# A kernel of two transformer blocks with an expert layer (PEER): which products the early expert tiles are made of, and which engine makes their rests

## The chip, the cores and the metric

The kernel runs on one core of a Trainium2 chip. Its time is the device time of one execution, in microseconds (us). Three executions of the kernel before took 1754.8 to 1755.04 us, median 1754.83.

## The reference, cut to what matters

Two blocks work on 256 tokens of width 1024. The second ends with an expert layer, PEER, which the change touches:

```python
q = (xb @ w_q).reshape(t, PEER_HEADS, 2, PEER_HALF)             # 8 heads, 2 halves of 128
s = jnp.einsum('thpd,hpkd->thpk', q, sub_keys)                  # 128 keys per half
top_s, top_i = lax.top_k(s, K)                                  # K = 16
cand_s = top_s[:, :, 0, :, None] + top_s[:, :, 1, None, :]
cand_i = top_i[:, :, 0, :, None] * PEER_N_KEYS + top_i[:, :, 1, None, :]
best_s, best_pos = lax.top_k(cand_s.reshape(t, PEER_HEADS, K * K), K)
idx = jnp.take_along_axis(cand_i.reshape(t, PEER_HEADS, K * K), best_pos, axis=-1)
gate = jax.nn.softmax(best_s, axis=-1)
h = jax.nn.gelu(jnp.einsum('thkd,td->thk', u_table[idx], xb), approximate=False)
return jnp.einsum('thk,thkd->td', gate * h, v_table[idx])
```

There are 128 x 128 = 16384 experts; all is float32.

## The kernel before, in words

The kernel doesn't gather rows of the tables. It multiplies all tokens with all of `u_table`, takes the gelu, multiplies by a weight that is zero for every expert that wasn't picked, and multiplies with all of `v_table`. Each table is cut into 128 tiles of 128 experts (512 KB each). This part, PEER, is the last: from about 975 us to the end at 1752 us.

**Exact products.** A float32 matrix is split into a top (rounded to the type fp32r, which TensorE takes at a high rate) and a rest (the matrix less its top). `three_passes` (L417) adds three products: top by top (L420), top by rest (L421), rest by top (L422). A tile of `u_table` so takes 8 x 3 matmuls of 128x256. The tokens' own top and rest are made once. A tile's pass through the engines is: SP starts its DMA into one of four slots of the ring (`expert_w`), ACT casts it to its top (`top_expert`, L2900), POOL (GpSimd) or DVE (VectorE) subtracts (the rest: L3113 on POOL, L3048 on DVE), PE (TensorE) multiplies, ACT takes the gelu from the bank into `hidden` (L2920; behind the hand-over L2927). SP starts the DMA of tile n when PE has begun tile n - 3; ACT casts tile n after the gelu of tile n - 3.

**Plain tiles.** Eight early tiles, `PLAIN` (6, 15, 17, 20, 30, 38, 41, 44), are multiplied as plain float32 matmuls (`plain_tile`, L2782), 8 of 128x256, without cast and rest. For them the tokens' rows are kept a second time, turned and not rounded: `x_turned`, made by 16 transposes of PE (L2771) and four copies of ACT (L2915), right behind the scores.

**The order of the stage.** PE first computes queries and scores (L2761), then the first `EARLY` = 46 tiles alone ("early tiles"). Meanwhile DVE picks, for each of two groups of 128 tokens (t = 0, 1; `pick_dve`): 16 heads of keys, five instructions each over 128 values (L2965 to L2969); a cast (L2978); the sums of all pairs (L2980, 128x2048); 8 heads of picks over 256 values; and for each of two digits of the picked position a shift or mask (L2988), a cast (L2989), an equality (L2990), a product (L2993) and a reduction (L2995), the last three over 2048 values. It ends with a copy (L2997), a subtraction (L2998) and, after t = 1, a memset (L3012) that posts `best_ready`.

**The hand-over.** `MERGED` is the order of the rest, written out as letters, and PE, ACT and DVE all follow it. "E": ACT, after the gelu of the last early tile, waits for `best_ready`, loads another table and takes the exponential (L2949). Then four more tiles "T"; "P": PE turns the picks and their weights (L2831) as soon as DVE has posted `picks_ready`, and ACT copies them; two tiles; then 64 groups "G" of four tokens, for which DVE makes masks (L3038, L3041), PE multiplies them (L2809) and DVE scales `hidden` (L3055), with the remaining tiles strewn between them. POOL makes the rests of the first `POOL_TILES` = `EARLY` + 6 tiles that aren't plain, DVE those of the others (L3048). Behind the last group, 128 tiles of `v_table` follow at 12 matmuls of 128x512 each.

**Buffers.** PSUM banks go round in two sets of four, `A` and `V`; `take` waits until a bank was emptied, `get` until it was filled. An engine's instructions run in the order written, so whatever waits holds up all behind it on that engine.

Of the kernel before, what the change touches and what calls it, by code (L numbers as in the profile page):

```python
# [14 lines left out]
ALU = mybir.AluOpType  # L15
ACT = mybir.ActivationFunctionType
F32 = mybir.dt.float32
# [5 lines left out]
P = 128  # L23
# [13 lines left out]
EARLY = 46  # L37
WEIGHT_UNIT = 2.0 ** 15
PLAIN = (6, 15, 17, 20, 30, 38, 41, 44)
# [156 lines left out]
def program(nc, dram, out, where):  # L196

    ctx = ExitStack()
    with ctx:
# [2465 lines left out]
        NH2 = 2 * PH  # L2665
# [29 lines left out]
        x_turned = hidden[:, EARLY + 6:EARLY + 14, :].rearrange("p j s -> p (j s)").rearrange("p (t k s) -> p t k s", t=TT, s=P)  # L2695
# [31 lines left out]
        def split_no(tile):  # L2727

            return tile + 1 - len([p for p in PLAIN if p < tile])
# [15 lines left out]
        def peer_pe(pe):  # L2745
# [21 lines left out]
            for t in range(TT):  # L2767
                for k in range(0, KT, 4):
                    bank = A.take(pe)
                    for j in range(4):  # L2770
                        ins = pe.transpose(bank[:, j * P:(j + 1) * P], xh[:, t, (k + j) * P:(k + j + 1) * P], ident)  # L2771
                    ins.then_inc(A.done, 1)
            mixed = Count()

            def plain_tile(tile):

                bank = A.take(pe)
                slot = tile % E_SLOTS
                pe.wait_ge(expert_landed[slot], 16 * (tile // E_SLOTS + 1))
                w = expert_w[:, slot, :].rearrange("p (k n) -> p k n", k=KT)  # L2780
                for k in range(KT):
                    ins = pe.matmul(bank[:, 0:S].rearrange("p (t s) -> p t s", t=TT), w[:, k, :], x_turned[:, :, k, :],  # L2782
                                    start=(k == 0), stop=(k == KT - 1))
                    if k == 0:
                        ins.then_inc(expert_begun, 1)
                ins.then_inc(A.done, 1)

            def u_tile(tile):
                bank = A.take(pe)
                slot = tile % E_SLOTS  # L2790
                if tile < POOL_TILES:
                    pe.wait_ge(u_split, split_no(tile))
                else:
                    pe.wait_ge(u_split_dve, tile - POOL_TILES + 1)
# [18 lines left out]
            for tile in range(EARLY):  # L2813
                if tile == PLAIN[0]:
                    A.evacuated_but(pe, 4)
                if tile in PLAIN:
                    plain_tile(tile)
                else:
                    u_tile(tile)
# [58 lines left out]
        def peer_act(act):  # L2878
# [9 lines left out]
            def top_expert():  # L2888

                n = tops.n  # L2890
                if tops.term is None and n in PLAIN:
                    tops.n += 1
                    return
# [76 lines left out]

        def pick_dve(dve, t):
            vec = nc.vector
            await_mark(dve, f"scores{t}")
            for h in range(NH2):
                ins = top16_dve(top_s[:, h, :], top_i[:, h, :], scores[:, t, h, :], spare_key[:, h, :])
            v(ins)
# [8 lines left out]
            v(ins)  # L2985

            for c, (op, by) in enumerate(((ALU.logical_shift_right, 4), (ALU.bitwise_and, 15))):
# [4 lines left out]
                                    ALU.is_equal))  # L2992
                v(vec.tensor_tensor(one_hot, one_hot, top_f[:, :, c, :].unsqueeze(2).broadcast_to([P, PH, TOPK, TOPK]),  # L2993
                                    ALU.mult))
                v(vec.tensor_reduce(key_no[:, t, c], one_hot, AX_X, ALU.add))  # L2995
# [6 lines left out]
        def peer_dve(dve):  # L3002
# [42 lines left out]
            def u_rest_dve(tile):  # L3045
                dve.wait_ge(expert_top_ready, split_no(tile))
# [61 lines left out]
        def peer_pool(pool):  # L3108
# [7 lines left out]
            for tile in range(POOL_TILES):  # L3116
                if tile not in PLAIN:
                    u_rest(tile)
# [196 lines left out]
```

## Time and profile before

| | |
|---|---|
| median of three runs | 1754.83 us |
| the profiled execution, its own time | 1754.11 us |
| its span | 1752.3 us |
| granted clock of TensorE | 0.996 of full |
| PE busy | 1703.8 us, 97% |
| DVE busy | 1134.7 us, 65% |
| ACT busy | 791.2 us, 45% |
| POOL busy | 348.8 us, 20% |
| matmuls | 12858 |
| chain of waits, by engine | PE 87%, DVE 5%, DMA 3%, ACT 2%, POOL 1% |

The span is the profiled execution from its first to its last instruction, 1.8 us shorter than its time. Busy times are per engine and may overlap. The chain of waits follows the work that ended last back to what released it. "Idle before" is the time that an engine stood before an instruction, with the one that ended it. A matmul row is pipelined: the next one begins before it ends, so the begin of a tile to the begin of the next is what a tile costs.

### The profile page before, as it was taken

How to read it: one execution, taken by the hardware profiler on the slowest of the kernel's cores; microseconds unless marked ns; L12 is line 12 of the kernel's file. 1: busy time of each engine (PE TensorE's matmuls, PEld its weight loads, DVE VectorE, ACT ScalarE, POOL GpSimd, SP SyncE). 2: the span in 40 equal slices, each digit the busy share in tenths (PEclk: the TensorE clock that was granted, in tenths of full speed). 3: DMA queues.
4: the chain of work that ended last, by engine and by line, in shares of the span. 5: the costliest groups of instructions: out<-in, count | busy, mean ns of one | idle time of the engine just before them, and what ended most of it. 6: DMA issues, size and time to landing. Idle time of an engine off the chain costs nothing.

```text
span 1752.3 us, 32963 instructions
## 1 busy us (share of the span) xinstructions
PE 1703.8 (97%) x12858; PEld 1514.6 (86%) x12858; DVE 1134.7 (65%) x1857; ACT 791.2 (45%) x1241; POOL 348.8 (20%) x325
## 2 busy tenths in 40 slices
PE   6999999999999999999899999999999999999997
PEld 2999879877999889877869999999999988888886
DVE  4877557677565465883664699488899644444444
ACT  4443445655544354551234534555544433333334
POOL 2000010111000010000010477600000155555553
PEclk9999999999999999999999999999999999999999
DMA  9878655456555534441044455545555566666664
GB/s 354 279 269 303 212 197 169 145 193 226 196 199 183 193 130 140 150 145 50 3 169 146 131 170 181 168 152 160 159 157 159 172 195 194 192 192 192 192 192 166
DMA packets 64385, 314.42 MB, mean 179 GB/s; under 512 B 7152, under 2 KB 7568, under 8 KB 44688
## 3 DMA queue, kind: packets, MB, share of 16 engines
q1 hardware_dynamic: 62928, 305.94, 52.3%
q10 hardware_dynamic: 1280, 6.82, 1.1%
q8 instruction: 85, 1.39, 0.3%
q14 instruction: 28, 0.23, 0.0%
q0 software_dynamic: 64, 0.04, 0.0%
HBM read 311.72 MB, written 1.05 MB: 178 GB/s over the span
## 4 chain that ended last, share of the span: by engine, by line
PE 87%; DVE 5%; DMA 3%; ACT 2%; POOL 1%; issue 1%; SPq 0%; DVEq 0%; POOLq 0%; ACTq 0%
PE bank L420 25%; PE bank L421 24%; PE bank L422 24%; DMA ring<-in_stream 2%; PE bank L2809 2%; DVE ring_rounded L381 1%; DMA ring<-in_experts 1%; POOL ring_rounded L3113 1%; PE bank L1351 1%; PE bank L2367 1%; PE bank L2782 1%; PE bank L781 1%; PE bank L2380 1%; PE bank L2018 1%; PE bank L595 0%
## 5 line engine op out<-in xcount | busy, mean ns | idle before, releaser
L422 PE MATMUL bank<-yb_rounded,ring_rounded 128*128 128x256 f32 x2000 | 566.4, 283 | 0.0
L2900 ACT CAST ring_rounded<-ring 128x1024 fp32r<-128x1024 f32 x248 | 260.5, 1051 | 279.2 <-DMA ring<-in_experts 279.2
L422 PEld LDWEIGHTS bank<-yb_rounded,ring_rounded 128*128 128x128 f32 x2000 | 384.2, 192 | 0.0
L381 DVE TENSOR_TENSOR ring_rounded<-ring,arena_rounded 128x1024 fp32r<-128x1024 f32 x230 | 270.8, 1220 | 132.6 <-ACT arena_rounded L367 132.0
L420 PE MATMUL bank<-yb_rounded,arena_rounded 128*128 128x256 f32 x1104 | 316.3, 287 | 1.7 <-DVE yT_rounded L897 1.3
L421 PE MATMUL bank<-yT_rounded,arena_rounded 128*128 128x256 f32 x1104 | 313.4, 284 | 0.0
L420 PE MATMUL bank<-yb_rounded,ring_rounded 128*128 128x256 f32 x960 | 278.2, 290 | 2.7 <-DVE ring_rounded L3048 1.7
L3075 DVE TENSOR_TENSOR ring_rounded<-ring,ring_rounded 128x1024 fp32r<-128x1024 f32 x128 | 156.8, 1225 | 190.5 <-ACT ring_rounded L2900 190.5
L367 ACT CAST arena_rounded<-ring 128x1024 fp32r<-128x1024 f32 x230 | 229.0, 1048 | 108.4 <-PE bank L420 99.8
L421 PE MATMUL bank<-yT_rounded,ring_rounded 128*128 128x256 f32 x960 | 271.2, 283 | 0.0
L421 PE MATMUL bank<-ring_rounded,arena_rounded 128*128 128x512 f32 x688 | 267.8, 389 | 0.0
L420 PEld LDWEIGHTS bank<-yb_rounded,arena_rounded 128*128 128x128 f32 x1104 | 212.9, 193 | 5.9 <-issue 4.0
L421 PEld LDWEIGHTS bank<-yT_rounded,arena_rounded 128*128 128x128 f32 x1104 | 212.9, 193 | 1.0 <-issue 1.0
L420 PE MATMUL bank<-ring_rounded,arena_rounded 128*128 128x512 f32 x512 | 199.4, 389 | 0.7 <-POOL arena_rounded L3131 0.7
L422 PE MATMUL bank<-ring_rounded,arena_rounded 128*128 128x512 f32 x512 | 199.3, 389 | 0.0
L420 PEld LDWEIGHTS bank<-yb_rounded,ring_rounded 128*128 128x128 f32 x960 | 183.6, 191 | 4.5 <-issue 4.3
L421 PEld LDWEIGHTS bank<-yT_rounded,ring_rounded 128*128 128x128 f32 x960 | 183.8, 191 | 0.1
L3128 POOL CAST arena_rounded<-field 128x256 fp32r (+1 forms) x128 | 94.7, 740 | 389.6 <-PE bank L420 389.6
L409 POOL TENSOR_TENSOR arena_rounded<-field,arena_rounded 128x1024 fp32r<-128x1024 f32 x8 | 23.0, 2896 | 704.8 <-ACT arena_rounded L401 704.8
L421 PEld LDWEIGHTS bank<-ring_rounded,arena_rounded 128*128 128x128 f32 x688 | 129.2, 188 | 27.2 <-issue 0.7
L3113 POOL TENSOR_TENSOR ring_rounded<-ring,ring_rounded 128x1024 fp32r<-128x1024 f32 x44 | 113.5, 2586 | 109.7 <-ACT ring_rounded L2900 109.6
L420 PEld LDWEIGHTS bank<-ring_rounded,arena_rounded 128*128 128x128 f32 x512 | 96.1, 188 | 21.1 <-issue 1.1
(439 smaller groups left out, 2651.4 us busy)
## 6 DMA issues: line engine op xcount, KB each, us to landing
ring<-in_stream SPq DMA_DIRECT2D x144, 1024.0 KB, 4.9
ring<-in_experts SPq DMA_DIRECT2D x256, 512.0 KB, 3.5
field<-in_stream SPq DMA_DIRECT2D x24, 512.0 KB, 7.1
field<-in_stream SPq DMA_DIRECT2D x4, 1024.0 KB, 6.9
field<-in_gains ACTq DMA_DIRECT2D x3, 512.0 KB, 7.8
field<-in_gains ACTq DMA_DIRECT2D x1, 1536.0 KB, 6.6
const<-in_const SPq DMA_DIRECT2D x1, 1473.0 KB, 11.2
xh<-in_x ACTq DMA_DIRECT2D x1, 1024.0 KB, 5.6
```

Of the source, the lines that this page charges most:

```text
L367: nc.scalar.copy(top, ring[:, g % SLOTS, half * HALF:(half + 1) * HALF]).then_inc(sem("weight_top_ready"), 1)
L381: ins = nc.vector.tensor_tensor(ring_r[:, g % SLOTS, half], ring[:, g % SLOTS, half], top.bitcast(F32), ALU.subtract)
L409: nc.gpsimd.tensor_tensor(rest[:, half], whole[:, half], top.bitcast(F32), ALU.subtract).then_inc(sem(f"own_split_{tag}"), 1)
L420: first = pe.matmul(bank, s_top, m_top, start=start, stop=False)
L421: pe.matmul(bank, s_top, m_rest, start=False, stop=False)
L422: return first, pe.matmul(bank, s_rest, m_top, start=False, stop=stop)
L781: ins = pe.matmul(bank[32 * k:32 * k + 32, :], silu_c[:, 4 * c + k, :], w[:, k, :], start=(c == 0), stop=(c == 1 and k > 0))
L2809: ins = pe.matmul(bank[:, q * P:(q + 1) * P], weighted[:, g % 2, q, i, :], masks[:, g % 2, q, 1, :], start=(i == 0), stop=(i == 1))
L2900: nc.scalar.copy(expert_top[:, n % E_SLOTS, :], expert_w[:, n % E_SLOTS, :]).then_inc(expert_top_ready, 1)
L3075: vec.tensor_tensor(expert_rest[:, slot, :], expert_w[:, slot, :], expert_top[:, slot, :].bitcast(F32), ALU.subtract).then_inc(v_split, 1)
L3113: nc.gpsimd.tensor_tensor(expert_rest[:, slot, :], expert_w[:, slot, :], expert_top[:, slot, :].bitcast(F32), ALU.subtract).then_inc(u_spl ...
L3128: nc.gpsimd.tensor_copy(h_top[:, b, :], src).then_inc(h_top_ready, 1)
```

## The change

It does four things.

1. `PLAIN`, `plain_tile`, `x_turned`, its 16 transposes and its four copies are gone. All 128 tiles of `u_table` go through `three_passes`.
2. Eight early tiles, `BETWEEN_PICKS` = (3, 9, 14, 19, 24, 30, 35, 41), have their rests made by DVE in `rest_between`, at fixed places in `pick_dve`: behind heads 4 and 14 of the keys, head 3 of the picks, the first equality and the second product of t = 0; behind head 7 of the keys, the sums and head 5 of the picks of t = 1. They have a semaphore of their own, for which PE waits. POOL makes the other rests.
3. `EARLY` is 48 and not 46, `POOL_TILES` 54 and not 52. POOL so makes 46 rests and not 44, DVE makes 74 and not 76 in the merged part.
4. ACT casts the eight tiles too. The counts for which rests wait become `tile + 1`.

Cut to its core (the counts in `v_rests` and `u_rest_dve`, and POOL's `tile not in PLAIN`, which becomes `tile not in BETWEEN_PICKS`, are left out):

```diff
-EARLY = 46
+EARLY = 48
-PLAIN = (6, 15, 17, 20, 30, 38, 41, 44)
+BETWEEN_PICKS = (3, 9, 14, 19, 24, 30, 35, 41)
...
-            for t in range(TT):
-                for k in range(0, KT, 4):
-                    bank = A.take(pe)
-                    for j in range(4):
-                        ins = pe.transpose(bank[:, j * P:(j + 1) * P], xh[:, t, (k + j) * P:(k + j + 1) * P], ident)
-                    ins.then_inc(A.done, 1)
...
-            def plain_tile(tile):
-
-                bank = A.take(pe)
-                slot = tile % E_SLOTS
-                pe.wait_ge(expert_landed[slot], 16 * (tile // E_SLOTS + 1))
-                w = expert_w[:, slot, :].rearrange("p (k n) -> p k n", k=KT)
-                for k in range(KT):
-                    ins = pe.matmul(bank[:, 0:S].rearrange("p (t s) -> p t s", t=TT), w[:, k, :], x_turned[:, :, k, :],
-                                    start=(k == 0), stop=(k == KT - 1))
...
             def u_tile(tile):
                 bank = A.take(pe)
                 slot = tile % E_SLOTS
-                if tile < POOL_TILES:
-                    pe.wait_ge(u_split, split_no(tile))
+                if tile in BETWEEN_PICKS:
+                    pe.wait_ge(sem("u_split_between"), BETWEEN_PICKS.index(tile) + 1)
+                elif tile < POOL_TILES:
+                    pe.wait_ge(u_split, pool_split_no(tile))
...
             for tile in range(EARLY):
-                if tile == PLAIN[0]:
-                    A.evacuated_but(pe, 4)
-                if tile in PLAIN:
-                    plain_tile(tile)
-                else:
-                    u_tile(tile)
+                u_tile(tile)
...
-            for t in range(TT):
-                for k in range(0, KT, 4):
-                    bank = A.get(act)
-                    nc.scalar.copy(x_turned[:, t, k:k + 4, :], bank[:, :].rearrange("p (j s) -> p j s", j=4)
-                                   ).then_inc(A.free, 1)
...
+        def rest_between(dve, tile):
+
+            dve.wait_ge(expert_top_ready, tile + 1)
+            slot = tile % E_SLOTS
+            nc.vector.tensor_tensor(expert_rest[:, slot, :], expert_w[:, slot, :], expert_top[:, slot, :].bitcast(F32),
+                                    ALU.subtract).then_inc(sem("u_split_between"), 1)
+
+        AFTER_KEYS = {(0, 4): 3, (0, 14): 9, (1, 7): 30}
+        AFTER_PICKS = {(0, 3): 14, (1, 5): 41}
+        AFTER_DIGITS = {(0, 0, "equal"): 19, (0, 1, "chosen"): 24}
...
             for h in range(NH2):
                 ins = top16_dve(top_s[:, h, :], top_i[:, h, :], scores[:, t, h, :], spare_key[:, h, :])
-            v(ins)
+                if h == NH2 - 1:
+                    v(ins)
+                if (t, h) in AFTER_KEYS:
+                    rest_between(dve, AFTER_KEYS[t, h])
...
+            if t == 1:
+                rest_between(dve, 35)
```

The order that this makes, at three places. PE, between the scores and the first expert tile; before (L2761 the scores, L2771 the transposes, L420 to L422 the first products of tile 0):

```order
L422 MATMUL bank<-yb_rounded,ring_rounded 128x256
L420 MATMUL bank<-yb_rounded,arena_rounded 128x256
L421 MATMUL bank<-yT_rounded,arena_rounded 128x256
L422 MATMUL bank<-yb_rounded,ring_rounded 128x256
L2761 MATMUL bank<-ring,field 128x128 x32
L2771 MATMUL bank<-const,xh 128x128 x16
L420 MATMUL bank<-yb_rounded,ring_rounded 128x256
L421 MATMUL bank<-yT_rounded,ring_rounded 128x256
```

In the changed kernel the row of L2771 is gone and nothing stands in its place. DVE, at the digits of t = 0, before (L2988 shift or mask, L2990 equality, L2993 product, L2995 reduction):

```order
L2988 TENSOR_SCALAR field<-field 128x128
L2989 CAST field<-field 128x128
L2990 TENSOR_TENSOR field<-field,const 128x2048
L2993 TENSOR_TENSOR field<-field 128x2048
L2995 TENSOR_REDUCE field<-field 128x128
L2988 TENSOR_SCALAR field<-field 128x128
L2989 CAST field<-field 128x128
L2990 TENSOR_TENSOR field<-field,const 128x2048
L2993 TENSOR_TENSOR field<-field 128x2048
L2995 TENSOR_REDUCE field<-field 128x128
L2997 COPY field<-field 128x8
```

The same place in the changed kernel, whose line numbers are 12 or 8 lower here; L2944 is the subtraction of `rest_between`:

```order
L2976 TENSOR_SCALAR field<-field 128x128
L2977 CAST field<-field 128x128
L2978 TENSOR_TENSOR field<-field,const 128x2048
L2944 TENSOR_TENSOR ring_rounded<-ring,ring_rounded 128x1024
L2983 TENSOR_TENSOR field<-field 128x2048
L2987 TENSOR_REDUCE field<-field 128x128
L2976 TENSOR_SCALAR field<-field 128x128
L2977 CAST field<-field 128x128
L2978 TENSOR_TENSOR field<-field,const 128x2048
L2983 TENSOR_TENSOR field<-field 128x2048
L2944 TENSOR_TENSOR ring_rounded<-ring,ring_rounded 128x1024
L2987 TENSOR_REDUCE field<-field 128x128
```

The first L2944 is the rest of tile 19, the second that of tile 24; each stands behind a wait for ACT's cast of its tile. The third place is head 5 of the picks of t = 1, in the changed kernel (L2934 to L2938 are the five instructions of a head):

```order
L2937 MAX field<-field 128x8
L2938 MAX_INDEX field<-field 128x8
L2944 TENSOR_TENSOR ring_rounded<-ring,ring_rounded 128x1024
L2934 MAX field<-field 128x8
L2935 MAX_INDEX field<-field 128x8
L2936 MATCH_REPLACE field<-field 128x256
L2937 MAX field<-field 128x8
```

That is the rest of tile 41. Behind it, to the end of the early tiles, DVE makes no rest; the digits of t = 1 stand as before.

## Rows read from the trace of the kernel before

**Rows 1.** The page, busy time, share of the span and instructions of each engine

```profile
PE 1703.8 (97%) x12858; PEld 1514.6 (86%) x12858; DVE 1134.7 (65%) x1857; ACT 791.2 (45%) x1241; POOL 348.8 (20%) x325
```

**Rows 2.** Waits of PE, 970 to 1752 us: who, for whom, total us, times, longest

```profile
PE bank L420 <- DVE ring_rounded L3048: 1.7, 1, 1.7
PE bank L420 <- POOL ring_rounded L3113: 0.7, 3, 0.3
```

**Rows 3.** Timeline of PE, 980 to 984 us: start, us, engine, line, operation

```profile
982.01 1.91 PE L2771 MATMUL bank<-const,xh 128*128 128x128 f32 x16
983.68 0.36 PE L420 MATMUL bank<-yb_rounded,ring_rounded 128*128 128x256 f32 x1
```

**Rows 4.** Timeline of ACT: gelus, begun as their tiles end, and a table load

```profile
989.71 0.38 ACT L2920 ACTIVATE field<-bank 128x256 f32<-128x256 f32 x1 [1.39 <-PE bank L422]
...
1001.23 0.38 ACT L2920 ACTIVATE field<-bank 128x256 f32<-128x256 f32 x1 [0.86 <-PE bank L422]
...
1010.43 0.38 ACT L2920 ACTIVATE field<-bank 128x256 f32<-128x256 f32 x1 [0.88 <-PE bank L422]
...
1013.70 0.38 ACT L2920 ACTIVATE field<-bank 128x256 f32<-128x256 f32 x1 [1.18 <-PE bank L422]
...
1059.06 0.38 ACT L2920 ACTIVATE field<-bank 128x256 f32<-128x256 f32 x1 [0.92 <-PE bank L422]
...
1061.94 0.38 ACT L2920 ACTIVATE field<-bank 128x256 f32<-128x256 f32 x1 [0.86 <-PE bank L422]
...
1124.68 1.28 ACT L2949 ACT_TABLE_LOAD   x1
...
1134.78 0.38 ACT L2927 ACTIVATE field<-bank 128x256 f32<-128x256 f32 x1 [0.79 <-PE bank L422]
```

**Rows 5.** Timelines of SP, ACT, POOL and PE: the life of tile 26

```profile
1053.56 0.33 SPq L3197 DMA_DIRECT2D ring<-in_experts  x1
...
1057.10 1.05 ACT L2900 CAST ring_rounded<-ring 128x1024 fp32r<-128x1024 f32 x1 [0.53 <-DMA ring<-in_experts]
...
1058.22 2.41 POOL L3113 TENSOR_TENSOR ring_rounded<-ring,ring_rounded 128x1024 fp32r<-128x1024 f32 x1 [0.30 <-ACT ring_rounded L2900]
...
1061.74 0.28 PE L420 MATMUL bank<-yb_rounded,ring_rounded 128*128 128x256 f32 x1
```

**Rows 6.** Timeline of DVE, 1026 to 1034 us: equality and product of the digits

```profile
1026.72 2.29 DVE L2990 TENSOR_TENSOR field<-field,const 128x2048 f32<-128x2048 f32 x1
1029.05 4.33 DVE L2993 TENSOR_TENSOR field<-field 128x2048 f32<-128x2048 f32 x1
```

**Rows 7.** Timeline of POOL, 1028 to 1041 us: the rests of tiles 16 and 19

```profile
1028.11 3.12 POOL L3113 TENSOR_TENSOR ring_rounded<-ring,ring_rounded 128x1024 fp32r<-128x1024 f32 x1 [3.29 <-ACT ring_rounded L2900]
...
1036.62 4.19 POOL L3113 TENSOR_TENSOR ring_rounded<-ring,ring_rounded 128x1024 fp32r<-128x1024 f32 x1 [0.88 <-ACT ring_rounded L2900]
```

**Rows 8.** DVE's digit and cast lines: times executed, duration ns min/median/max

```profile
L2993 DVE TENSOR_TENSOR field<-field x4: 2291/3310/4371, 1029.0 to 1105.8; 128x2048 f32<-128x2048 f32 x4
...
L2988 DVE TENSOR_SCALAR field<-field x4: 226/1038/2314, 1026.2 to 1100.9; 128x128 uint32<-128x128 uint32 x4
...
L2989 DVE CAST field<-field x4: 227/228/230, 1026.5 to 1103.2; 128x128 f32<-128x128 uint32 x4
...
L2997 DVE COPY field<-field x2: 170/1210/2249, 1045.3 to 1110.4; 128x8 f32<-128x8 f32 x2
...
L2978 DVE CAST field<-field x2: 293/686/1079, 1004.7 to 1071.1; 128x256 f32<-128x256 uint32 x2
```

**Rows 9.** Timeline of DVE: where its picking begins, and its last instruction

```profile
979.52 0.29 DVE L2965 MAX8 field<-field 128x8 f32<-128x128 f32 x1 [11.91 <-ACT field L2908]
...
1113.08 0.06 DVE L3012 MEMSET small<- 128x1 f32 x1
```

**Rows 10.** Waits of all engines, 975 to 1145 us: VectorE's for the exponential

```profile
DVE field L3015 <- ACT field L2949: 13.3, 1, 13.3
```

**Rows 11.** Line L3048, rests of merged tiles on DVE: duration ns min/median/max

```profile
L3048 DVE TENSOR_TENSOR ring_rounded<-ring,ring_rounded x76: 1212/1215/1227, 1142.0 to 1387.4; 128x1024 fp32r<-128x1024 f32 x76
```

More of the change, by code:

```diff
@@ L2692, in program @@
         denom = take(TT * PH).rearrange("p (t h) -> p t h", t=TT)
-        x_turned = hidden[:, EARLY + 6:EARLY + 14, :].rearrange("p j s -> p (j s)").rearrange("p (t k s) -> p t k s", t=TT, s=P)
         pick_weights = field[:, HID:HID + S]
@@ L2725, in program, with pool_split_no @@
         MERGED = ["E"] + ["T"] * 4 + ["P"] + ["T"] * (BEFORE - 4)
-        def split_no(tile):
-            return tile + 1 - len([p for p in PLAIN if p < tile])
+        def pool_split_no(tile):
+            return tile + 1 - len([p for p in BETWEEN_PICKS if p < tile])
         for m in range(GROUPS):
@@ L2890, in top_expert @@
                 n = tops.n
-                if tops.term is None and n in PLAIN:
-                    tops.n += 1
-                    return
                 full = 16 * (n // E_SLOTS + 1)
@@ L2984, in pick_dve @@
                 ins = top16_dve(best[:, t, h, :], pos[:, h, :], flat[:, h, :], spare_sum[:, h, :])
-            v(ins)
+                if h == PH - 1:
+                    v(ins)
+                if (t, h) in AFTER_PICKS:
+                    rest_between(dve, AFTER_PICKS[t, h])
             for c, (op, by) in enumerate(((ALU.logical_shift_right, 4), (ALU.bitwise_and, 15))):
@@ L2992, in pick_dve @@
                                     ALU.is_equal))
+                if (t, c, "equal") in AFTER_DIGITS:
+                    rest_between(dve, AFTER_DIGITS[t, c, "equal"])
                 v(vec.tensor_tensor(one_hot, one_hot, top_f[:, :, c, :].unsqueeze(2).broadcast_to([P, PH, TOPK, TOPK]),
                                     ALU.mult))
+                if (t, c, "chosen") in AFTER_DIGITS:
+                    rest_between(dve, AFTER_DIGITS[t, c, "chosen"])
                 v(vec.tensor_reduce(key_no[:, t, c], one_hot, AX_X, ALU.add))
@@ L3045, in u_rest_dve @@
             def u_rest_dve(tile):
-                dve.wait_ge(expert_top_ready, split_no(tile))
+                dve.wait_ge(expert_top_ready, tile + 1)
                 slot = tile % E_SLOTS
@@ L3073, in v_rests @@
                 mixed.n += 1
-                dve.wait_ge(expert_top_ready, mixed.at(NKEY - len(PLAIN) + mixed.n))
+                dve.wait_ge(expert_top_ready, mixed.at(NKEY + mixed.n))
                 vec.tensor_tensor(expert_rest[:, slot, :], expert_w[:, slot, :], expert_top[:, slot, :].bitcast(F32),
@@ L3111, in u_rest @@
                 slot = tile % E_SLOTS
-                pool.wait_ge(expert_top_ready, split_no(tile))
+                pool.wait_ge(expert_top_ready, tile + 1)
                 nc.gpsimd.tensor_tensor(expert_rest[:, slot, :], expert_w[:, slot, :], expert_top[:, slot, :].bitcast(F32),
@@ L3116, in peer_pool @@
             for tile in range(POOL_TILES):
-                if tile not in PLAIN:
+                if tile not in BETWEEN_PICKS:
                     u_rest(tile)
```

3 lines of the change are left out of this document (removed).

## The prediction

> **What bounds the kernel now.** I read the page's busy times first, then PE's waits, then the timelines of the early tiles. PE is busy 97% of the span [rows 1], and from 970 us to the end it waits for little: 1.7 us once for DVE's first rest of the merged part, 0.7 us for POOL [rows 2]. So PE's own work is the time, and what is taken off it counts in full as long as nobody becomes late. Two gelus that follow each other without a stall show what a tile of three passes costs: 1061.94 - 1059.06 = 2.88 us [rows 4].
>
> How much room the others have shows in the life of tile 26 [rows 5]: DMA issued 1053.56, cast from 1057.10 for 1.05, rest on POOL from 1058.22 for 2.41, done 1060.63; PE begins the tile at 1061.74. Its slack is 1.1 us. POOL has 2.4 us of work per 2.88 us. Whatever delays a rest by over 1.1 us stalls PE.
>
> **What delays rests: POOL and DVE shut each other out.** DVE's equality runs 1026.72 to 1029.01 [rows 6]. POOL's rest begun at 1028.11 takes 3.12 and not 2.4, to 1031.23, 2.2 after the equality's end [rows 7]. DVE's product, begun at 1029.05, takes 4.33 and not 2.29, to 1033.38, which is 2.15 after POOL's end. Whoever comes second stands until the other's whole instruction is over, and they take turns. DVE's smaller one-source instructions stand too: shift or mask 0.23 or up to 2.31, copy 0.17 or 2.25, cast over 256 values 0.29 or 1.08; two of four products are 2.0 too long, like rest 19 on POOL with 4.19 [rows 7, 8]. Summed, DVE stood for POOL six times, 2.04 + 2.08 + 1.62 + 2.08 + 2.08 + 0.79 = 10.7 us.
>
> **The sum, part by part** (against the profiled execution's 1754.1 us).
>
> Gone from PE: the transposes, 983.68 - 982.01 = 1.67 us [rows 3]. ACT's four copies behind them go too; ACT had room, so 0.
>
> Plain against three passes: the gelus at 1001.23 and 1010.43 enclose plain tile 6 and two others, 9.20 us, where three tiles of 2.88 take 8.64 [rows 4]. So 0.56 each, 8 of them: 4.5 us. Off PE in all: 6.2 us.
>
> Stalls that may go: between the gelus of tiles 1 and 49, at 989.71 and 1134.78, lie 48 tiles and 145.1 us; 48 x 2.88 + 8 x 0.56 = 142.7. The difference, 2.3 us with the roundings, is stalls (tile 9's gelu at 1013.70 comes 3.27 after the one before it) [rows 4].
>
> The two tiles that become early, with POOL's two more rests and DVE's two fewer in the merged part, leave PE's work as it is: 0. DVE's single wait of 1.7 us sits behind "P", whose order is unchanged: it stays.
>
> So with nobody late: 1754.1 - 6.2 - 2.3 = 1745.6.
>
> Added to DVE: eight rests of 1.22 [rows 11] = 9.8 us. DVE picks from 979.52 to 1113.1 [rows 9] and then waits 13.3 us [rows 10], so this alone fits. But a rest takes two tensors from SBUF like the equality and the product, so I count it as one that POOL shuts out; no row has such a rest meet POOL. And the plain tiles 15, 17, 20 and 41, 44 are gone, in whose time POOL stood idle beside DVE's digits. I work it forward: tile n due at 982.0 + 2.88 n plus earlier stalls; DMA issued 0.5 behind the begin of tile n - 3 and landing 3.5 later as for tile 26; cast 1.05; rest 2.4; turns as above.
>
> - Keys and sums of t = 0: rests 3 and 9 come in time. DVE's cast stands 2.3 for POOL's rest 10 (before: 0.8), the sums then hold up rest 11: tile 11 stalls 1.1.
> - First digit: before, the equality began at 1026.7 [rows 6]. Now three rests (3.6), a wait for a cast (0.4), the longer cast wait (1.5) and a turn of POOL (2.5) come first: 1034.6. Rest 19 runs 1036.9 to 1038.1, tile 19 was due at 1037.8: stall 0.3, and tile 21 0.9.
> - Second digit: product 1038.1, waits 2.2, ends 1042.5; reduction 1044.8; mask and cast stand a turn of 2.2 each, 1049.8; equality 1052.1; product 1054.5; rest 24 stands 2.2 and ends 1057.9. Tile 24 was due at 1053.3: **stall 4.4**.
> - t = 1: rest 30 in time, rest 35 late by 1.2, rest 41 in time.
> - Digits of t = 1, no tile spared: where equality and product follow each other, a rest takes 2.3 + 2.2 = 4.5 per 2.88. Less the slack for the first: about 1.0 + 1.5 for each digit, 5.0.
> - DVE's own turns there make six waits of 2.2. It ends at 1139.3, 26.2 later than before: 9.8 of rests, 1 of waits for casts, 15.4 more for POOL. ACT, at 1124.7 for "E" before [rows 4], gets there at about 1133.9 and stands 5.4 us; its cast of tile 51 is behind it. 1.3 of it is absorbed, since ACT is three tiles ahead: tile 51 stalls 4.1.
>
> New stalls: 1.1 + 0.3 + 0.9 + 4.4 + 1.2 + 5.0 + 4.1 = 17.0. 1745.6 + 17.0 = 1762.6, and 0.5 for ten restarts of PE, 1763.1: 9.0 more than before. The three runs' median is 0.7 above the profiled time, so I forecast 1763.8.
>
> Bounds. If neither rests nor small instructions stand for POOL any more than before, 1747 (the last rival). If the DMAs land later (4.5 us) or rest 35 too meets POOL (2.2 more), 1766 to 1769. The cast L2989 never met POOL, four times 0.23 [rows 8]; I take it like the longer cast, which did. The Trainium skill, "Advanced Engine Details and Errata", section "Mode Summary", says that GpSimd and two-port VectorE instructions block each other and lists casts among the latter; by it the sum stays, and if L2989 didn't stand it would be 0.9 less.
>
> **The rivals.** A difference under 0.2%, 3.5 us, is about what a measurement of this kernel can't tell from none.
>
> *Fewer turns (0.12).* DVE's small instructions slip in between POOL's instead of standing for each. For it: in rows 8 half of them took 0.23. Against: they met nobody then. Without their waits DVE is some 10 us earlier, rest 24 is nearly in time and "E" hardly waits: new stalls of 12, +3 to +5, 1758.
>
> *Relief and new stalls cancel (0.10).* The change doesn't do what it says: moving rests to DVE does not relieve, since each still takes the same turn, but the stalls stay near 8.5 us. 1752 to 1758, say 1755. Trainium skill, "Perfetto Trace Analysis", section "Optimizing Scalar/DVE Operations": as the two share a read port, offloading between them "might not help".
>
> *Faster (0.14).* The places are just right. Shift DVE's places of before by 1.2 us per rest already made, and each of the eight falls between its tile's cast and 1.3 us before its tile is due (rest 19: 1029.0 + 3.7 = 1032.7, cast 1032.8, needed 1036.7). Then POOL is idle in the widest meetings, DVE's waits stay at 10.7 us, it ends at 1123.5, "E" waits 1 to 2 us: 1745.6 + 2 = 1747.5. It decides at tile 24: DVE has 2.5 us of room there, one extra turn of 2.2. A second one flips it. Against: my working finds four by then.
>
> **How the numbers follow.** The forecast case, +5 to +15, has 0.64; of fewer turns about two thirds are over +3.5. Slower: 0.64 + 0.08 = 0.72; same 0.13; faster 0.15. The range 1752 to 1769 holds the forecast case up to its late DMAs, fewer turns and most of the cancelling case; the fast case is left out.
>
> **What would show it.** Right: product (now L2983) and casts of 2.2 us and more, over ten of them; DVE's rest for tile 24 taking 3.4 and not 1.22 or begun behind 1052; PE waits for DVE L2944 and POOL of 15 us in all; DVE waiting for the exponential not 13.3 us but next to nothing, and ACT waiting for DVE at L2949's place; `best_ready`'s memset near 1139. First products at 982.0 and no L2771 confirm the 1.7; gelus 2.88 apart where nobody stalls the 4.5. Wrong: the memset near 1123, DVE's waits near 10 us, and PE's stalls under 4 us; then the time is 1747, and the step that failed is the count of turns.

## The result, and the profile after

The changed kernel takes **1764.36 us** (median of 5 runs, 1762.31 to 1767.11) beside 1754.8 for the kernel before on the same chip: ratio 1.0053, 95% interval 1.0041 to 1.0064, slower by 9.3 us (7.2 to 11.2). The forecast was 1763.8. The profiled execution was the slowest of the five: it took 1767.11, its span is 1763.9.

The page's busy times of the change, beside [rows 1]:

```profile
PE 1702.9 (97%) x12906; PEld 1517.3 (86%) x12906; DVE 1155.7 (66%) x1861; ACT 797.1 (45%) x1243; POOL 358.5 (20%) x327
```

PE is busy 0.9 us less than before, though more than that was taken off it: busy time also grows where its clock is low, so what a part costs is read from the starts of tiles below. What grew are waits. The waits of the changed kernel, 970 to 1180 us (engine, its instruction, whom it waited for, total us, times, longest), beside [rows 2, 10]:

```profile
PEld bank L420 <- issue: 12.5, 6, 4.1
PE bank L420 <- POOL ring_rounded L3105: 8.5, 6, 2.4
...
ACT field L2918 <- DVE small L3004: 4.3, 1, 4.3
PE bank L420 <- DVE ring_rounded L2944: 3.9, 1, 3.9
DVE ring_rounded L2944 <- ACT ring_rounded L2874: 3.2, 3, 1.3
...
PE bank L420 <- DVE ring_rounded L3040: 1.8, 1, 1.8
...
DVE field L3007 <- ACT field L2918: 0.5, 1, 0.5
```

PE waits 8.5 us for POOL where it waited 0.7, and 3.9 for one rest of DVE (L2944 is `rest_between`). DVE's 13.3 us of waiting for the exponential are 0.5, and ACT waits 4.3 for DVE. The rows don't add up to a cost: a stall shows on PE and on its weight loads both. So from here on a **stall** is read from PE's timeline: the start of a tile, less that of the tile before, less 2.88 us.

DVE's lines of the picking in the change (busy us, mean ns of one, idle before), where [rows 8] had means of 1154 for the shift and 228 for the cast, as L2988 and L2989:

```profile
L2983 DVE TENSOR_TENSOR field<-field 128x2048 f32<-128x2048 f32 x4 | 15.5, 3873 | 0.1
L2944 DVE TENSOR_TENSOR ring_rounded<-ring,ring_rounded 128x1024 fp32r<-128x1024 f32 x8 | 11.8, 1474 | 3.3 <-ACT ring_rounded L2874 3.2
L2976 DVE TENSOR_SCALAR field<-field 128x128 uint32<-128x128 uint32 x4 | 9.5, 2370 | 0.1
...
L2963 DVE TENSOR_TENSOR field<-field 128x2048 f32<-128x2048 f32 x2 | 6.7, 3334 | 0.1
L2977 DVE CAST field<-field 128x128 f32<-128x128 uint32 x4 | 5.2, 1292 | 0.1
L2989 DVE COPY field<-field 128x8 f32<-128x8 f32 x2 | 2.4, 1216 | 0.1
```

All four shifts and masks stood a whole turn of POOL. The timeline of DVE around the digits of t = 0 (start us, us) shows the chain of turns that ends in tile 24, and the last instruction of the picking:

```profile
1045.38 2.35 DVE L2976 TENSOR_SCALAR field<-field 128x128 uint32<-128x128 uint32 x1
1047.77 2.38 DVE L2977 CAST field<-field 128x128 f32<-128x128 uint32 x1
1050.18 2.29 DVE L2978 TENSOR_TENSOR field<-field,const 128x2048 f32<-128x2048 f32 x1
1052.51 2.29 DVE L2983 TENSOR_TENSOR field<-field 128x2048 f32<-128x2048 f32 x1
1054.83 3.25 DVE L2944 TENSOR_TENSOR ring_rounded<-ring,ring_rounded 128x1024 fp32r<-128x1024 f32 x1
...
1141.50 0.06 DVE L3004 MEMSET small<- 128x1 f32 x1
```

And PE's timeline at tile 24, which waits for that rest of 3.25 us:

```profile
1054.01 0.28 PE L422 MATMUL bank<-yb_rounded,ring_rounded 128*128 128x256 f32 x1
1058.23 0.55 PE L420 MATMUL bank<-yb_rounded,ring_rounded 128*128 128x256 f32 x1 [3.94 <-DVE ring_rounded L2944]
1058.58 0.41 PE L421 MATMUL bank<-yT_rounded,ring_rounded 128*128 128x256 f32 x1
1058.80 0.41 PE L422 MATMUL bank<-yb_rounded,ring_rounded 128*128 128x256 f32 x1
```

The matmuls behind the idle come 0.21 to 0.22 us apart and not 0.12. The stretches show why (length, busy time of PE, PEld, DVE, ACT, POOL, then PE's granted clock):

```profile
1058.20:1063.50 5.30, 5.27 (x25) 5.30 (x26) 5.03 (x17) 0.00 (x0) 2.12 (x1) 0.50 0.32 102
1063.50:1070.00 6.50, 6.50 (x55) 6.50 (x55) 6.06 (x33) 3.14 (x5) 3.58 (x2) 0.99 0.53 161
```

Tile 24 ran at a clock of 0.50, 1.2 GHz, took 5.26 us, and tile 25 had the full clock again. Idle 3.94 us, PE lost 2.4 more.

The chain of waits between 1030 and 1145 us, its shares by line, is headed by a line of DVE's; in the kernel before, PE's L420 led there with 16.4% and the highest of DVE's had 1.2%:

```profile
by line: DVE field L2983 13.4%; PE bank L420 11.4%; PE bank L422 10.7%; PE bank L421 10.7%; DVE field L2976 8.3%; DVE field L2978 8.0%; DMA ring<-in_experts 7.7%; DVE field L2987 6.0%; DVE ring_rounded L2944 5.0%; DVE field L2977 4.5%; ACT 
```

**The ledger** of the two profiled executions. The products of the scores start at 974.86 before and 975.37 after (0.5 us of difference, ahead of what was changed). With 46 early tiles in place of 48, the kernel before has done two more groups (L2809, 0.50 us each) when it starts tile 54; they are taken off, so that both sides have done the same.

| term | predicted | found |
|---|---|---|
| transposes, first expert product behind the scores' start | -1.67 | 8.81 to 7.07: -1.7 |
| eight tiles of three passes | -4.5 | -4.5 |
| old stalls gone | -2.3 | -2.4 |
| tile 11 | 1.1 | 1.4 |
| tiles 19, 21 | 0.3, 0.9 | 0.1, 0.9 |
| tile 24, the wait | 4.4 | 4.1 |
| tile 24, the clock | none | 2.4 |
| tile 35 | 1.2 | 0.6 |
| tiles 44, 45, 48, 49 | 5.0 | 5.5 |
| tile 51 ("E") | 4.1 | 2.5 |
| restarts, stalls under 0.1 | 0.5 | 0.6 |
| up to the start of tile 54 | +9.0 | +9.4 |
| behind the start of tile 54 | 0 | +1.7 |

0.5 + 9.4 + 1.7 are the 11.6 us between the two spans; the two executions' times are 13.0 apart, the medians of the runs 9.6. So the ledger has more to explain than the medians show.

Most of the last row can be read from the trace. PE at the start of tile 54 in the change, and at tile 52 before, which stands at the same place of the order; then the stretches of the two tiles:

```profile
1159.02 0.39 PE L420 MATMUL bank<-yb_rounded,ring_rounded 128*128 128x256 f32 x1 [1.83 <-DVE ring_rounded L3040]
```
```profile
1143.36 0.36 PE L420 MATMUL bank<-yb_rounded,ring_rounded 128*128 128x256 f32 x1 [1.75 <-DVE ring_rounded L3048]
```
```profile
1159.00:1163.40 4.40, 4.38 (x24) 4.40 (x24) 3.72 (x5) 0.00 (x0) 0.00 (x0) 0.61 0.36 119
```
```profile
1143.30:1146.30 3.00, 2.94 (x25) 2.93 (x25) 2.96 (x5) 0.26 (x1) 0.00 (x0) 1.00 0.49 131
```

Both stand there for DVE's first rest of the merged part, but in the change the clock then fell: from this tile to the next are 4.86 us, before 3.37. That is 1.5 of the 1.7.

### The profile page after: what moved, and what is told of

Read it like the earlier page. It is cut to its first block, busy times and chain, and to the rows that moved or that the text cites. A ratio compares the mean times of both kernels' runs of the same rounds, so it can differ in the third digit from the quotient of the medians.

```text
span 1763.9 us, 33078 instructions
## 1 busy us (share of the span) xinstructions
PE 1702.9 (97%) x12906; PEld 1517.3 (86%) x12906; DVE 1155.7 (66%) x1861; ACT 797.1 (45%) x1243; POOL 358.5 (20%) x327
## 4 chain that ended last, share of the span: by engine, by line
PE 84%; DVE 10%; DMA 3%; ACT 2%; issue 1%; POOL 0%; SPq 0%; DVEq 0%; POOLq 0%; ACTq 0%
PE bank L420 24%; PE bank L421 23%; PE bank L422 23%; DMA ring<-in_stream 2%; PE bank L2791 2%; DVE ring_rounded L381 1%; DMA ring<-in_experts 1%; DVE field L2983 1%; PE bank L1351 1%; PE bank L2367 1%; PE bank L781 1%; PE bank L2380 1%; DVE field L2976 1%; DVE field L2978 1%; PE bank L2018 1%
## 5 line engine op out<-in xcount | busy, mean ns | idle before, releaser
L422 PE MATMUL bank<-yb_rounded,ring_rounded 128*128 128x256 f32 x2064 | 586.2, 284 | 0.0
L2874 ACT CAST ring_rounded<-ring 128x1024 fp32r<-128x1024 f32 x256 | 268.9, 1051 | 294.6 <-DMA ring<-in_experts 294.6
L422 PEld LDWEIGHTS bank<-yb_rounded,ring_rounded 128*128 128x128 f32 x2064 | 398.4, 193 | 0.0
L420 PE MATMUL bank<-yb_rounded,arena_rounded 128*128 128x256 f32 x1104 | 316.7, 287 | 1.6 <-DVE yT_rounded L897 1.3
L420 PE MATMUL bank<-yb_rounded,ring_rounded 128*128 128x256 f32 x1024 | 297.4, 290 | 15.2 <-POOL ring_rounded L3105 8.5
L421 PE MATMUL bank<-yT_rounded,ring_rounded 128*128 128x256 f32 x1024 | 291.0, 284 | 0.0
L420 PEld LDWEIGHTS bank<-yb_rounded,arena_rounded 128*128 128x128 f32 x1104 | 213.5, 193 | 5.3 <-issue 3.8
L420 PEld LDWEIGHTS bank<-yb_rounded,ring_rounded 128*128 128x128 f32 x1024 | 197.7, 193 | 17.0 <-issue 12.5
L420 PE MATMUL bank<-ring_rounded,arena_rounded 128*128 128x512 f32 x512 | 199.3, 389 | 0.7 <-POOL arena_rounded L3123 0.7
L422 PE MATMUL bank<-ring_rounded,arena_rounded 128*128 128x512 f32 x512 | 199.2, 389 | 0.0
L421 PEld LDWEIGHTS bank<-yT_rounded,ring_rounded 128*128 128x128 f32 x1024 | 197.9, 193 | 0.0
L3105 POOL TENSOR_TENSOR ring_rounded<-ring,ring_rounded 128x1024 fp32r<-128x1024 f32 x46 | 123.2, 2690 | 114.7 <-ACT ring_rounded L2874 114.4
L420 PEld LDWEIGHTS bank<-ring_rounded,arena_rounded 128*128 128x128 f32 x512 | 96.1, 188 | 21.3 <-issue 1.1
```

Source lines behind the costliest of these rows:

```text
L420: first = pe.matmul(bank, s_top, m_top, start=start, stop=False)
L421: pe.matmul(bank, s_top, m_rest, start=False, stop=False)
L422: return first, pe.matmul(bank, s_rest, m_top, start=False, stop=stop)
L2874: nc.scalar.copy(expert_top[:, n % E_SLOTS, :], expert_w[:, n % E_SLOTS, :]).then_inc(expert_top_ready, 1)
L3105: nc.gpsimd.tensor_tensor(expert_rest[:, slot, :], expert_w[:, slot, :], expert_top[:, slot, :].bitcast(F32), ALU.subtract).then_inc(u_spl ...
```

## The experiments

Unless it is said otherwise each is the changed kernel with one edit. Baselines of a batch are the kernel before on the same chip (1755.64, 1754.87 and 1756.05 us in the three batches), so ratios are compared.

**1. No rest on DVE** (`e1_none`): are the eight rests a relief or a load?

```diff
-BETWEEN_PICKS = (3, 9, 14, 19, 24, 30, 35, 41)
+BETWEEN_PICKS = ()
```
with the eight calls of `rest_between` taken out.

> The changed kernel without DVE's eight rests: POOL makes the rests of all 54 tiles, DVE only picks. Theory (turns at a shared port): each of the eight rests cost DVE 1.2 us and left the turns of the others as they were, so taking them away must not cost time. DVE's memset that posts best_ready comes near 1129 instead of 1141, ACT no longer stands at the exponential, tiles 24 and 35 are late for DVE no more; POOL's rests inside equality and product still take 4.4. By the same forward working as in the prediction 1760 (1758 to 1762). Rival (the eight rests are real relief for a POOL that is too slow): slower than the changed kernel, 1767 or more. Rival (only DVE's added load at the hand-over counts): 1761.

Measured: 1763.95 us, ratio 1.0049 (1.0033 to 1.0064), above the 1758 to 1762 that I expected. Neither: the eight rests on DVE are worth nothing that can be told. They do take turns away, since without them DVE stood 33.6 us for POOL and not 26.0, but they cost DVE 9.8 us of their own and 3.2 of waits. So its memset comes 161.2 us behind the scores' start beside 166.1, and not the 12 us sooner that I expected. In the profile PE's stalls are 13.1 us, where the change had 18.0, nearly all on POOL's rests, and no tile runs at half clock.

**2. Digits in PSUM** (`e2_psum`): take away what POOL shuts out.

```diff
-        top_f = take(NH2 * TOPK).rearrange(...)
+        digit_bank = V.banks[3]
+        top_f = digit_bank[:, 0:256].rearrange(...)
-        digit_u = take(NPICK).bitcast(U32)...
+        digit_u = digit_bank[:, 256:384].bitcast(U32)...
-        digit_f = take(NPICK)...
+        digit_f = digit_bank[:, 384:512]...
```

> The changed kernel with three small tensors of the digits (shifted digits, their float copies, the key numbers as floats; 512 columns in all) in a free PSUM bank instead of SBUF. Then shift, cast, equality and product each read or write PSUM and have at most one tensor in SBUF to read; number, order and sizes of all instructions are the same. Theory (turns at a port of SBUF): shift, cast, equality and product take their uncontended 0.2 to 2.4 us each, POOL's rests beside them 2.4; DVE's memset near 1126; PE's stalls in this stage fall from about 17 to 3 us: 1749 (1747 to 1753). Rival (DVE and POOL are simply late by their own load): no change, 1764. Rival (the DMAs land later, since more tiles are cast): no change, 1763.

Measured: 1755.01, ratio 1.0 (0.999 to 1.001): 9.4 us less than the change, and not the 15 that I expected. The lines of shift, cast and product (ns min/median/max):

```profile
L2977 DVE TENSOR_SCALAR bank<-field x4: 295/295/295, 1030.5 to 1116.5; 128x128 uint32<-128x128 uint32 x4
```
```profile
L2978 DVE CAST bank<-bank x4: 299/299/300, 1030.8 to 1116.8; 128x128 f32<-128x128 uint32 x4
```
```profile
L2984 DVE TENSOR_TENSOR field<-field,bank x4: 2280/2286/2286, 1034.6 to 1119.5; 128x2048 f32<-128x2048 f32 x4
```

With one operand out of SBUF no shift, cast, equality or product stood. The sums (4.34 us once) and the copy (1.49 and 2.26), which the edit left in SBUF, still did. (The Trainium skill, "VectorE: DVE Perf Modes", section "Why PSUM operands drop a tier", says that a PSUM operand excludes the mode that needs both SBUF ports; by it shift and cast should no longer meet POOL, and the rows agree.) What is left sits elsewhere: DVE, now early, waited 8.1 us for casts in front of its rests, then came late to rest 35, which took 3.25 us, and PE stood before tile 35 and ran it at half clock, 3.8 + 2.4 us. That leaves my 1747 to 1753 missed.

**3. Six more early tiles** (`e3_early54`): was the exponential behind DVE's end the bound?

```diff
-EARLY = 48
+EARLY = 54
```

> The changed kernel with EARLY = 54 instead of 48, so that ACT comes to the exponential six tiles later. Theory: only the stall behind the hand-over goes (tiles 51 and 52, 3.2 us); all the others stay, and the rests of tiles 49 to 59 on POOL meet no digits: 1761 (1760 to 1762). Rival (the late picks are the whole loss): 1750. ACT's wait for DVE's memset is 0 in both.

Measured: 1764.76, ratio 1.0053 (1.0034 to 1.0072). A miss: I expected 1761. DVE waits 14.5 us for ACT again and tile 51's stall is gone, yet the time is the same; the 4.0 us before tile 24 stay. The profiled stage, from the scores to the end, was 3.5 us shorter than that of the change, the medians show none of it; this run doesn't settle what tile 51 costs.

**4. POOL writes but doesn't read** (`e4_memset`): is it POOL's reading?

```diff
+                if tile < POOL_TILES and tile not in BETWEEN_PICKS:
+                    rest = top
...
-                nc.gpsimd.tensor_tensor(expert_rest[:, slot, :], ...)
+                if seen["pool"]:
+                    pool.wait_ge(u_split, seen["pool"])
+                seen["pool"] += 1
+                nc.gpsimd.memset(field[:, 60 * S:60 * S + 2750], 0.0)
```

This kernel is for timing alone: it leaves out the product of rest by top for 46 tiles, so its result is not the reference's.

> The changed kernel in which POOL makes no rests: in place of each it sets 2750 unused columns to zero, about 2.4 us, so POOL is as busy and posts as late, but reads nothing; PE multiplies the top once more in place of the rest for those tiles (left out: rest by top for the 46 tiles of POOL). Theory, with the port being one for reading: DVE's products, sums and rests no longer stand for POOL, and POOL not for them. The shift, cast and copy, which write SBUF from one source, may still stand, as four instructions did for a memset of POOL at 7 us. 1754 (1750 to 1758) if those stand, 1748 if they don't either. Rival (any busy POOL instruction shuts DVE out): 1764. Rival (load): 1764.

Measured: 1751.51, ratio 0.9977 (0.9966 to 0.9988), inside the range for standing small instructions. POOL's work, DVE's product and DVE's shift in it:

```profile
L3111 POOL MEMSET field<- x46: 2390/2395/2404, 977.0 to 1133.5; 128x2750 f32 x46
```
```profile
L2985 DVE TENSOR_TENSOR field<-field x4: 2287/2292/2294, 1037.0 to 1117.5; 128x2048 f32<-128x2048 f32 x4
```
```profile
L2978 DVE TENSOR_SCALAR field<-field x4: 372/1370/1976, 1031.6 to 1113.8; 128x128 uint32<-128x128 uint32 x4
```

POOL is as busy as before, but instructions with two SBUF inputs run free beside it, while the one-input shift still stands (0.23 alone), like the copy (1.74 and 1.60 for 0.17) and one cast of 256 values (2.48 for 0.29). So two kinds of meeting exist: two inputs against POOL's reading, and small one-input instructions against POOL's writing too. (The Trainium skill, "SBUF — State Buffer", section "Who interferes with whom", draws this line: a DVE instruction with two SBUF inputs contends with a POOL instruction that reads SBUF and not with one that only writes it, and shifts, casts and copies contend when they run in a mode that takes both ports. The trace agrees.)

**5. Rest 24 one step earlier** (`e6_hook24`, and `e11_hook24_early54` with 54 early tiles): what is the big stall worth?

```diff
-        AFTER_DIGITS = {(0, 0, "equal"): 19, (0, 1, "chosen"): 24}
+        AFTER_DIGITS = {(0, 0, "equal"): 19, (0, 1, "equal"): 24}
```

> The change with DVE's rest 24 made one step earlier, behind the equality in place of the product. Theory A (PE's stalls add up): the stall of 4.1 us before tile 24 falls to about 1.8, and with the shorter idle tile 24 runs at the full clock (2.88 us and not 5.26), together -4.7: 1759.7 us. Theory B (DVE's picking sets the time to tile 51: in the change and with no rest on DVE PE began tile 54 17.5 and 17.4 us behind the memset): the clock and the stall at 24 are repaired, but the memset stays at 166 us behind the scores' start, tile 51 waits some 4 to 5 us longer than 2.5, and the time stays at 1763 to 1765. I hold B for likelier. That the slow tile has nothing to do with the idle before it: it still takes 5.26.

> The same move of rest 24, with 54 early tiles in place of 48, so that ACT is at the exponential six tiles later and DVE's end binds nobody (DVE then waits for ACT by over 10 us). If the stall and the slow tile 24 cost their own length where DVE doesn't set the end, this is 4 to 5 us under the change with 54 early tiles (1764.8): 1760 (1758 to 1762). If the time is set by something else, the same as it: 1764 to 1765.

Measured: 1767.34, ratio 1.0072 (1.0058 to 1.0085), and 1765.3, ratio 1.0056 (1.0043 to 1.0069). Nothing gained in either: the first is slower than both theories had it, the second like the change with 54 early tiles (1.0053). Tile 24 waits no more and runs at full clock, but the loss is back at DVE's next rest, tile 30, with the same half clock behind it. PE there, and the stretch of tile 30, in `e6_hook24`:

```profile
1077.20 0.56 PE L420 MATMUL bank<-yb_rounded,ring_rounded 128*128 128x256 f32 x1 [5.66 <-DVE ring_rounded L2944]
```
```profile
1077.20:1082.00 4.80, 4.80 (x22) 4.80 (x23) 4.46 (x25) 0.00 (x0) 0.00 (x0) 0.50 0.38 114
```

The start of DVE's rest 30 in the change and in this run:

```profile
1074.49 1.23 DVE L2944 TENSOR_TENSOR ring_rounded<-ring,ring_rounded 128x1024 fp32r<-128x1024 f32 x1 [0.97 <-ACT ring_rounded L2874]
```
```profile
1074.99 2.06 DVE L2944 TENSOR_TENSOR ring_rounded<-ring,ring_rounded 128x1024 fp32r<-128x1024 f32 x1
```

Counted from the scores' start DVE begins it at 99.1 and at 100.2 us: it gets there at its own pace, whatever PE saved, and here it met POOL too. So both theories as I wrote them were wrong in the place: stalls don't add up, but it isn't DVE's end that takes them back, it is its next rest. In `e11_hook24_early54` DVE's end bound nobody (it waited 13.5 us for ACT), and tile 30 waited 7.1 us.

**6. Rest 35 ahead of the sums, with digits in PSUM** (`e7_psum_35`): the same mending on the PSUM version.

```diff
+        AFTER_KEYS = {(0, 4): 3, (0, 14): 9, (1, 7): 30, (1, 14): 35}
-            if t == 1:
-                rest_between(dve, 35)
```

> The digits' small tensors in PSUM, and DVE's rest 35 made ahead of the sums (behind the 15th key of t = 1) in place of behind them, where it took 3.25 us for 1.22, left PE idle for 3.8 us and was followed by a tile of 5.26 us. If these two are what was left of the loss: -6.1 + 0.8 for the rest 36 that POOL makes beside the sums: 1750 us (1748 to 1751), under the kernel before. If DVE's end takes over (memset at 153.3 + 17.4 = 170.7 against PE's 174.5 at tile 54): 1751 to 1752, with tile 51 waiting 1 to 2 us longer. If neither stood in the way, no change from 1755.0.

Measured: 1755.92, ratio 1.0 (0.999 to 1.0011). A miss: no gain. Tile 35 starts on time, but tile 37 waits 1.4 us for POOL, and again the stall went to DVE's next rest: rest 41 takes 3.33 us, and tile 41 waits 3.0 us and runs at half clock.

**7. Tiles that fit DVE's pace** (`e13_late54` with SBUF digits and 54 early tiles, `e12_psum_fit` with digits in PSUM): the same places in DVE's order, but for rest 34 of the second, which stands just ahead of the sums, and other tile numbers. Of the first and of the second:

```diff
-BETWEEN_PICKS = (3, 9, 14, 19, 24, 30, 35, 41)
+BETWEEN_PICKS = (3, 9, 14, 20, 26, 33, 39, 45)
```
```diff
-BETWEEN_PICKS = (3, 9, 14, 19, 24, 30, 35, 41)
+BETWEEN_PICKS = (3, 9, 14, 19, 23, 29, 34, 41)
```
with the same numbers in `AFTER_KEYS`, `AFTER_PICKS` and `AFTER_DIGITS` (left out).

> The change with its turns in SBUF as they are and 54 early tiles, but DVE's eight rests at the same places of its order made for later tiles, which its slow pace meets: 3, 9, 14, 20, 26, 33, 39, 45. Theory: in the change PE is held to DVE's pace at each such rest (rest 24 repaired, the 5 us came back at rest 30), so with tiles that DVE meets in time no PE wait for DVE's rests stays and no slow tile, while POOL's stalls at 44 to 49 stay: 1759 us (1757 to 1761) beside 1764.8 with 54 early tiles and the old places. Rival: POOL's turns alone hold PE; it gets the 5 us back as stalls on POOL's rests: 1763 to 1765.

> The change with the digits' small tensors in PSUM and DVE's eight rests at the same places of its order, but for tiles 3, 9, 14, 19, 23, 29, 34 and 41: those whose cast has ended and whose turn hasn't come when DVE gets there (rest 34 one step ahead of the sums). If what was left in the two PSUM runs (DVE waiting 8.1 and 5.2 us for casts, then PE 3.8 and 3.0 us for DVE, each with a slow tile of 5.26) is the misfit of the places, both waits go, no tile runs at half clock, and the time is 1749 us (1748 to 1751) beside 1755.0 and 1755.9. If the places can't be met and the misfit only moves on once more, 1754 to 1756.

Measured: `e13_late54` 1758.01, ratio 1.0014 (1.0003 to 1.0024), against 1.0053 with the old tile numbers: 0.39% of 1755, 6.8 us, as expected. PE's waits in it, 970 to 1180 us:

```profile
PE bank L420 <- POOL ring_rounded L3105: 6.6, 6, 1.3
PE bank L420 <- DVE ring_rounded L3040: 1.8, 1, 1.8
PE bank L420 <- ACT field L2889: 1.4, 3, 0.5
```

No wait for L2944, though two of DVE's rests still met POOL (2.40 and 3.28 us): they had room. And DVE stood 31.0 us for POOL in it, more than the change's 26.0. So the turns are all there and most of the loss is gone: what they cost depends on whether a tile waits behind them. `e12_psum_fit`: 1750.7, ratio 0.997 (0.9961 to 0.998), 5.3 us under the kernel before, inside the expected range. Its rests on DVE, all at their bare length, and PE's waits:

```profile
L2945 DVE TENSOR_TENSOR ring_rounded<-ring,ring_rounded x8: 1205/1225/1227, 987.5 to 1099.2; 128x1024 fp32r<-128x1024 f32 x8
```
```profile
PE bank L420 <- POOL ring_rounded L3104: 3.2, 3, 1.1
PE bank L420 <- DVE ring_rounded L3039: 1.6, 1, 1.6
```

**8. Digits in PSUM with no rest on DVE, or two** (`e5_none_psum`, `e14_psum_two`): the edits of 1 and 2 together; and with

```diff
+BETWEEN_PICKS = (9, 32)
+        AFTER_KEYS = {(0, 14): 9, (1, 15): 32}
```

> The change with no rest on DVE (POOL makes all 54) and with the digits' small tensors in PSUM. My theory: the turns in the digits made the change slow, the eight rests on DVE relieve nothing. Then only the two sums (up to 4.4 us) still meet POOL, picking gives its memset some 140 us behind the start of the scores (166.1 in the change, 153.3 with PSUM and the rests, 161.2 with neither), new stalls of PE come to 3 us or less, and the time is about 1749 us (1746 to 1751), 6 below the kernel before. Rival: the rests on DVE do relieve POOL once the digits are out of its way; then this is slower than the change with PSUM digits (1755.0), 1756 to 1759, with stalls of over 9 us on POOL's rests.

> Digits' small tensors in PSUM and only two rests on DVE, each just ahead of the sums of a token half (tiles 9 and 32), where POOL's rest took 4.35 and 3.93 us in the run with none, and PE then stood 1.95 and 1.2 us at tiles 9 and 31. If these two meetings are the rest of its loss: 1749 us (1748 to 1750) beside 1751.05. If the delay passes to the next of POOL's rests (tiles 10, 11, 33): 1750.5 to 1752.

Measured: `e5_none_psum` 1751.05, ratio 0.9981 (0.9972 to 0.999); DVE's memset 131.1 us behind the scores' start, PE's stalls 5.0 us, two more than expected, and the time at the upper end of what I expected. The rival fails: without DVE's rests it is not slower than run 2 (ratio 1.0), which has all eight at the old places, but some 3 us faster. `e14_psum_two` 1749.89, ratio 0.9967 (0.9956 to 0.9978): **5.8 us under the kernel before**, the fastest whole kernel here; stalls 3.1 us. Its lead over `e12_psum_fit` and `e5_none_psum` lies within or near the intervals.

**9. The kernel before, with only its digits in PSUM** (`e8_before_psum`, the diff of 2 on the kernel before).

> The kernel before, with only the digits' small tensors in PSUM: the eight plain tiles, the turned rows and POOL's 44 rests stay. In the change the same edit was worth 9.4 us. If those turns did harm only where the change had taken the plain tiles away (PE's stalls of before come to 2.4 us in all, and DVE waits 13.3 us for ACT at its end), this gives 1 to 2 us: 1753 to 1754 beside 1754.9, with the memset some 9 us sooner than 138.2 and DVE's wait for the exponential longer by as much. Rival: the edit is worth as much here, 1746 to 1748; then three passes for all tiles never paid.

Measured: 1753.59, ratio 0.9989 (0.9978 to 1.0), some 2 us, at the edge of what can be told; memset at 132.7, DVE waits 17.3 us for ACT, stalls 0.9 us where it had 2.4. So the turns hardly hurt while plain tiles lay between. Against it `e14_psum_two` (ratio 0.9967 to 0.9989) is 3.9 us faster: by the two profiles three passes for all tiles bring 6.2 us of work less 2.2 more of stalls (3.1 against 0.9), 4.0, once most turns are gone.

## Why the prediction was right, step by step

**What bounds.** Right: PE's work fell by what the two terms said, -1.67 and 8 x 0.56, and the whole loss is waits and, behind two of them, a lowered clock.

**The count of turns**, on which it all hung. DVE stood 26 us in the change: over their bare times the four shifts and masks 8.6, the products 6.3, two casts of L2977 4.3, the sums 2.1, rest 24 2.0, a copy 2.1 and L2961 0.6. I had 10.7 + 15.4 = 26.1. Twelve waits of 2 us or more; I said over ten. The memset came at 1141.5, predicted 1139.3: the 2.2 more are waits for casts, 3.2 and not 1. L2977, which had never met POOL, did so twice. That these turns are a cause is shown by run 2, which removes most of them and 9.4 us. One meeting came otherwise than worked out: at t = 0 it was not the cast (L2961, 0.29) but the sums (4.38) that stood, and tile 11 was late all the same, 1.4 for 1.1.

**Tile 24.** Rest 24 takes 3.25 (I said 3.4) and tile 24 waits 4.1 (4.4). PE's waits for L2944 and POOL, which I had put at 15 us in all, are 3.9 and 8.5. What the step lacked is the clock: the tile behind the idle ran at 0.50, 2.4 us more.

**"E".** ACT in the change:

```profile
1135.97 1.28 ACT L2918 ACT_TABLE_LOAD   x1
1141.60 0.42 ACT L2918 ACTIVATE field<-field 128x256 f32<-128x256 f32 x1 [4.34 <-DVE small L3004]
```

ACT was there at 1135.97, not 1133.9. It loads the table first and waits behind it, not ahead of it as the text on the kernel before has it, so 1.28 of the 5.6 us to the exponential (I had 5.4) cost nothing new, and 4.3 were left. Tile 51 stalled 2.5, not 4.1: ACT's lead took up 1.8 and not 1.3, from a smaller delay. This term was 1.6 too large. Clock and "E" nearly offset each other, so the sum to tile 54, 9.4 against 9.0, is closer than its terms.

**Behind the start of tile 54**, where I had put nothing, lie 1.7 us, and 1.5 of them are that tile at a lowered clock. The tile at this place of the order takes 4.86 to 4.89 us to the next in the change, in all three runs with 54 early tiles and in `e8_before_psum`, and 3.37 in the kernel before and in the other runs. Counted as in the ledger, these other runs with 48 early tiles still have 0.4 to 1.1 there. That remainder is open, and so is what decides whether the clock falls.

**Luck in the number.** The sum, 1763.1, was made for a profiled execution. That one took 1767.11: the clock at two tiles, 3.9 us, the 0.5 ahead of what was changed and 1.4 more outside the span weren't in it, and the smaller "E" gave back 1.6. The forecast meets the median, 1764.36, more closely than the sum meets the execution that it describes.

**The rivals.** *Fewer turns* fell by the 26 us. *Cancelling* was right in part: rests on DVE bring no net relief (run 1: 1763.95 beside 1764.36). But it isn't that each still takes the same turn; they save 7.6 us of turns and cost DVE 13.0. It was wrong in its number, since the stalls didn't stay at 8.5. *Faster* needed DVE within 2.5 us at tile 24, and that was the right point: where DVE's pace does fit, with the digits in PSUM, `e12_psum_fit` gives 1750.7.

**What the prediction did not see** is the tie that runs 5 to 7 showed. I added stalls as if each were worth its length. But each rest on DVE holds PE to DVE's pace (PE can't pass the tile) and DVE to PE's (the cast comes three tiles ahead at most), so a stall mended at one was paid at the next in all three tries (`e6_hook24`, `e11_hook24_early54`, `e7_psum_35`).

## What to carry to other kernels

An engine's spare time is not free for work that shares a port with the engine it relieves: count the turns, not the busy time, ask for each which tile waits behind it, and look first for operands that can sit in PSUM. Work put at fixed places of another engine's order ties both engines at each place; choose what it works on from the pace that this engine has with the change in it, and after mending one stall look at the next tie before believing the gain. A long idle of TensorE can cost more than its length.

## What the runs showed of the hardware that I had not expected

**The clock after an idle.** PE idled 3.94 us in the change, 3.60 in `e2_psum`, 5.66 in `e6_hook24`, 6.96 in `e11_hook24_early54` and 2.82 in `e7_psum_35`; each time the next 24 matmuls took 5.26 us. In `e3_early54` they took 4.44 after 3.89. After 2.36 us of idle before tile 51 they took 2.95 in the change and 4.43 in `e6_hook24`. Before the first rest of the merged part PE idles 1.6 to 1.9 us in nearly every profile: after 1.79 to 1.86 the next tile was 1.5 us longer in five of them, and not in `e7_psum_35` after 1.86. So the same idle can cost 0 or 1.5 us, and nothing here tells which.

**Who waits for whom** between DVE and POOL depends on what POOL reads, as run 4 shows. And a meeting costs both: in the change POOL's longest rest took 4.43 us, where a bare one takes 2.4, about what it takes to let one DVE instruction of 2.29 pass.
